# A diffusion block in f32 on one core: router and convolution rows transposed from normalized rows, the norm's affine part folded into columns, one product behind instead of two

## The chip, the core and the metric

The kernel runs on one core of one Trainium2 chip. Its engines work side by side, each through its own instructions in order, and wait for each other on semaphores: TensorE (matrix products and transposes), VectorE, ScalarE, GpSimd, and SyncE, which here only starts DMA transfers. The metric is the time of one execution on the device, in microseconds (us). The median of three runs of the kernel before is 2563.14 us (2562.48 to 2564.69). A measurement of this kernel can't tell a difference below some 0.2% from none.

## The reference

Two layers over 1024 tokens (and 256 context tokens in the first) of 1024 values, all f32. Cut to what the change touches:

```python
def layer_norm(x, w, b):            # mean and variance over the 1024 values of a row
    return (x - mu) * rsqrt(var + LN_EPS) * w + b

for l in range(2):
    u = modulate(h, m[0], m[1])                       # u = h * scale + shift, per column
    y = attn_gla_mixer(u, ...) if l == 0 else short_conv_mixer(u, ...)     # ends in @ w_out
    h = post_norm(h, m[2] * y, ln_w[l, 0], ln_b[l, 0])   # layer_norm(ALPHA*h + m[2]*y, w, b)
    tokens = modulate(h, m[3], m[4])
    y = hier_moe(tokens, router..., moe_w1, moe_w3, moe_w2)   # top 1 of 4 groups, top 2 of its 8 experts
    h = post_norm(h, m[5] * y, ln_w[l, 1], ln_b[l, 1])
```

The mixer of layer 1 is a gated convolution over three tokens: `u @ w_in`, the convolution, `@ w_out`. The router is a product of the modulated tokens with 4 + 32 columns. The two chosen experts of each token (w1, w3, w2 of 512 hidden values) are computed for gathered tokens; the weights of all experts, 6 MB each, stream in once per layer.

## The kernel before

The 1024 tokens are 8 tiles of 128 rows (t = 0 to 7). A product needs its input transposed, with the values on partitions: eight 128x128 transposes per tile on TensorE (line 585), then eight copies out of PSUM, which apply a scale and a shift per column (which is then per partition): ScalarE does four (`modulated`, line 1124), VectorE the other four (line 1367). "Columns" below means these eight.

The order of work on each engine is written out by hand, in one block per engine, and the engines meet in semaphores that count up. Those of this change:
- `out_mm`: output product of a tile done. `res`: residual written. `nrm`: rows normalized (mean and deviation applied, no weight and bias yet). `ln`: affine part applied too, rows stored in `hh`. `tile_T`: transposes done. `tile_a`, `tile_d`: columns done on ScalarE, VectorE. `comb`: combine products of a tile done. `wa2_in`: a group of small loads of the prologue.

Prologue. SyncE loads the adaLN weights in pieces (`ada_part`), VectorE sums them (line 1409), TensorE transposes the sums between units of the first projection. Small loads (convolution taps, sinks) stand in the same queue ahead of `ada_part(18)`.

Output product of layer 0 (`mixed_product`) and of layer 1 (`odd_product`). Per tile 32 passes of 128x512 (13.8 us). VectorE multiplies by the gate (line 1612), adds ALPHA times the input (1614), takes statistics of both halves (1594, 1595) and combines them (1597). ScalarE takes the root (1250), VectorE makes scale and shift (1602, 1604), ScalarE normalizes (1252). GpSimd multiplies by the norm's weight (1976) and adds its bias (1978) into `hh`, counts `ln`. TensorE transposes tile t - 2 in the middle of the product of tile t (`rows_T`) and multiplies with the router (`logits`, lines 880 and 882) at its end. Behind the loop stand the transposes and logits of tiles 6 and 7. SyncE writes each tile of `hh` to DRAM after its `ln`, then loads the next norm's parameters and the first 16 pieces of expert weights (1 MB each; 12 at once, four after the routing's order is known).

Routing and experts. VectorE computes the routing from the logits (lines 1620 to 1755) with some products on TensorE. GpSimd then gathers the rows of the first two blocks by indirect DMA (line 1987) from DRAM. TensorE transposes them and goes through 22 blocks, while SyncE refills weight pieces in slots that a block has freed.

Combine (`combined`) after the experts: per tile ALPHA times the saved rows plus the two experts' rows, by products with diagonal matrices (lines 1074 and 1076), then statistics on VectorE out of PSUM, the norm on ScalarE, the affine part on VectorE (`affine`, lines 1832 and 1834). In layer 0 the tile is then transposed and put through columns for the convolution (`stream_T`), tile t - 2 behind the combine of tile t. In SyncE's order, right after the combine's loads:

```python
sp.wait_ge(S("ln"), 2 * NT)     # all 8 tiles of the combine's affine
ln_params(1, 0)
router(1)
# then the convolution's weights wc, 2 x 3 loads of 512 KB; the first conv_chunk waits for them
```

`hh` lies in bigC, the rows between residual and norm in bigA (`zt0`, `zt1`; `zt` for the combine).

## Time and profile before

| | |
|---|---|
| median of 3 runs | 2563.14 us |
| profiled execution | 2561.24 us, its span 2559.4 us |
| TensorE busy | 2331.6 us, 91% of the span |
| VectorE, ScalarE, GpSimd busy | 30%, 16%, 11% |
| DMA while experts run | up to 421 GB/s over most slices |
| chain that ended last | TensorE 73%, DMA 12%, VectorE 7% |
| TensorE's clock over the span | 0.957 of full |

A busy share over the span says little here, since every stretch has its own limit. The chain of waits tells what a stretch hangs on: each row of it is a start, a length and the work that was waited for. The stretches that matter for the change: prologue (0 to 180 us), output product of layer 0 (630 to 784), routing (784 to 828), combine of layer 0 (1364 to 1431), output product of layer 1 (1775 to 1923), routing (1923 to 1968), final combine (2500 to 2559).

### The profile page before, as it was taken

How to read it: one execution, taken by the hardware profiler on the slowest of the kernel's cores; microseconds unless marked ns; L12 is line 12 of the kernel's file. 1: busy time of each engine (PE TensorE's matmuls, PEld its weight loads, DVE VectorE, ACT ScalarE, POOL GpSimd, SP SyncE). 2: the span in 40 equal slices, each digit the busy share in tenths (PEclk: the TensorE clock that was granted, in tenths of full speed). 3: DMA queues.
4: the chain of work that ended last, by engine and by line, in shares of the span. 5: the costliest groups of instructions: out<-in, count | busy, mean ns of one | idle time of the engine just before them, and what ended most of it. 6: DMA issues, size and time to landing. Idle time of an engine off the chain costs nothing.

```text
span 2559.4 us, 28344 instructions
## 1 busy us (share of the span) xinstructions
PE 2331.6 (91%) x10480; PEld 1179.1 (46%) x10480; DVE 759.8 (30%) x1661; ACT 418.6 (16%) x912; POOL 277.7 (11%) x341
## 2 busy tenths in 40 slices
PE   7989999998993999999998799997994999999887
PEld 3556448886553344344343344443553343443332
DVE  2783125555336111111115111111335111111115
ACT  2301324442111111011013100000120101101011
POOL 0000103222221100000000000000221000000000
PEclk9999999999995999999999899998995999999998
DMA  9871000002127999999965210101017999999956
GB/s 387 326 296 38 1 0 2 2 2 83 52 74 295 367 421 415 416 393 421 421 280 209 68 49 27 47 25 66 33 45 302 421 421 413 417 404 421 421 217 246
DMA packets 135165, 572.24 MB, mean 224 GB/s; under 512 B 24153, under 2 KB 49913, under 8 KB 82554
## 3 DMA queue, kind: packets, MB, share of 16 engines
q1 hardware_dynamic: 121786, 536.92, 52.8%
q0 software_dynamic: 13248, 33.57, 3.4%
q8 instruction: 82, 1.34, 0.2%
q14 instruction: 49, 0.40, 0.0%
HBM read 549.47 MB, written 35.65 MB: 229 GB/s over the span
## 4 chain that ended last, share of the span: by engine, by line
PE 73%; DMA 12%; DVE 7%; issue 3%; SPq 2%; ACT 1%; POOL 1%; DVEq 0%; POOLq 0%; ACTq 0%
PE bank L988 19%; PE bank L1060 13%; PE bank L1010 9%; DMA bigA<-in_moe_w 8%; PE bank L628 8%; PE bank L898 4%; PE bank L920 4%; PE bank L731 3%; DVE lnwb L1409 2%; PE bank L585 2%; SPq L406 2%; PE bank L882 1%; DMA bigA<-in_ada_w 1%; PE bank L745 1%; PE bank L714 1%
## 5 line engine op out<-in xcount | busy, mean ns | idle before, releaser
L988 PE MATMUL bank<-bigA,bigB 128*32 128x512 f32 (+2 forms) x1968 | 468.2, 601 | 12.6 <-DMA bigA<-in_moe_w 8.9
L1060 PE MATMUL bank<-bigB,bigA 128*128 128x512 f32 x768 | 331.5, 595 | 10.9 <-DMA bigA<-in_w_in_odd 10.9
L628 PE MATMUL bank<-bigC,bigB 128*128 128x512 f32 (+3 forms) x768 | 292.6, 537 | 0.0
L1010 PE MATMUL bank<-bigA,bigB 128*32 128x512 f32 (+2 forms) x1120 | 271.3, 601 | 18.6 <-DMA bigA<-in_moe_w 15.9
L988 PEld LDWEIGHTS bank<-bigA,bigB 128*32 128x32 f32 (+2 forms) x1968 | 162.4, 137 | 252.1 <-issue 246.7
L988 PE MATMUL bank<-bigC,bigB 128*128 128x512 f32 (+2 forms) x720 | 264.1, 597 | 8.8 <-DMA bigA<-in_moe_w 5.6
L1060 PEld LDWEIGHTS bank<-bigB,bigA 128*128 128x128 f32 x768 | 146.8, 191 | 195.2 <-issue 195.2
L628 PEld LDWEIGHTS bank<-bigC,bigB 128*128 128x128 f32 x768 | 142.8, 193 | 127.7 <-issue 119.7
L1124 ACT ACTIVATE bigB<-bank,small 128x128 f32<-128x128 f32 x288 | 107.2, 459 | 434.9 <-PE bank L585 434.8
L1010 PEld LDWEIGHTS bank<-bigA,bigB 128*32 128x32 f32 (+2 forms) x1120 | 98.9, 140 | 163.6 <-issue 159.4
L988 PEld LDWEIGHTS bank<-bigC,bigB 128*128 128x128 f32 (+2 forms) x720 | 91.0, 151 | 132.0 <-issue 128.0
L1992 POOL DMA_INDIRECT y_rows<-bigB,ints x44 | 44.3, 1007 | 904.8 <-DVE bigB L1784 904.8
L1784 DVE TENSOR_TENSOR bigB<-bank,gate 128x512 f32<-128x512 f32 x88 | 56.7, 686 | 268.0 <-PE bank L1010 268.0
L1775 DVE TENSOR_TENSOR bigB<-bigB,bank 128x512 f32<-128x512 f32 x44 | 30.2, 687 | 327.3 <-PE bank L988 327.3
L898 PE MATMUL bank<-bigB,bigA 128*128 128x512 f32 x256 | 114.2, 602 | 13.0 <-DMA bigB<-in_w_out_odd 13.0
L920 PE MATMUL bank<-bigB,bigA 128*128 128x512 f32 x256 | 115.2, 605 | 8.1 <-issue 8.1
L1266 ACT ACTIVATE bigB<-bank 128x512 f32<-128x512 f32 x44 | 26.3, 597 | 551.5 <-PE bank L988 551.5
L1976 POOL TENSOR_TENSOR bigA<-bigA,lnwb 128x1024 f32<-128x1024 f32 x16 | 37.6, 2347 | 648.2 <-ACT bigA L1252 648.2
L1876 DVE TENSOR_TENSOR bigA<-bank,bigA 128x512 f32<-128x512 f32 x16 | 11.1, 692 | 294.5 <-ACT bigA L1341 294.5
L1779 DVE COPY bigB<-bank 128x256 f32<-128x256 f32 x44 | 18.6, 424 | 267.0 <-PE bank L996 267.0
L1409 DVE SCALAR_TENSOR_TENSOR lnwb<-bigA,normw,lnwb 128x1024 f32<-128x1024 f32 x70 | 89.9, 1284 | 7.5 <-DMA bigA<-in_ada_w 3.3
L731 PE MATMUL bank<-bigB 128*128 128x128 f32 x608 | 83.8, 284 | 7.6 <-issue 6.6
(269 smaller groups left out, 2274.6 us busy)
## 6 DMA issues: line engine op xcount, KB each, us to landing
bigA<-in_moe_w SPq DMA_DIRECT2D x292, 1024.0 KB, 20.8
bigC<-in_moe_w SPq DMA_DIRECT2D x92, 1024.0 KB, 22.2
bigA<-in_ada_w SPq DMA_DIRECT2D x40, 1024.0 KB, 7.7
bigA<-y_rows SPq DMA_DIRECT2D x16, 1024.0 KB, 4.9
bigA<-in_w_in_odd SPq DMA_DIRECT2D x24, 512.0 KB, 6.1
bigA<-in_ada_w SPq DMA_DIRECT2D x4, 2048.0 KB, 12.4
bigA<-in_x SPq DMA_DIRECT2D x16, 512.0 KB, 11.1
bigC<-in_w_in_even SPq DMA_DIRECT2D x4, 2048.0 KB, 14.1
```

What stands on the lines that cost most here:

```text
L406: sp.dma_start(dst, src, **how).then_inc(S(name), 16)
L585: last = tp(bank(b + k // 4)[:, (k % 4) * P:(k % 4 + 1) * P], cols(src, n)[:, k, :], ident)
L628: last = mm(bank(n % 3)[:, 0:w], uT[:, k, t * P:(t + 1) * P], wring[:, g % 2, k, at_:at_ + w], start=(k == 0), stop=(k == KC - 1))
L731: last = mm(dst, sc[:, p % 3, g, k * P:(k + 1) * P], unit_p[:, p % 2, g, :], start=True, stop=True, skip_group_check=True)
L898: last = mm(bank(2 * (t % 2) + n), zT[:, k, t * P:(t + 1) * P], wout1[:, k, n * 512:(n + 1) * 512], start=(k == 0), stop=(k == KC - 1))
L920: last = mm(bank(2 * (t % 2) + n), lhs[:, k, :], wout[:, k0 + k, n * 512:(n + 1) * 512], start=(k0 + k == 0), stop=(k0 + k == KC - 1), ski ...
L988: last = mm(bank(m)[at_:at_ + w, :], xT[:, j, KC // 2 * h + k, at_:at_ + w], w13_at[SLOT_OF[m, h, q][0]][:, k, :], start=(h == 0 and k == ...
L1010: last = mm(bank(6 + n)[at_:at_ + w, :], gT[:, 2 * h + k, at_:at_ + w], w2_at[SLOT_OF[2, h, q][0]][:, k, n * 512:(n + 1) * 512], start=(h ...
L1060: last = mm(bank(3 * half + m), wc[:, j, m, k, :], u1T[:, k, half * 512:(half + 1) * 512], start=(k == 0), stop=(k == KC - 1))
L1124: last = go(dst[:, k, :], bank(b + k // 4)[:, (k % 4) * P:(k % 4 + 1) * P], ACT.Identity, bias=shift[:, k:k + 1], scale=scale[:, k:k + 1])
L1409: V(v.scalar_tensor_tensor(acc[:, r % 2], part, cond[:, k, 0:1], acc[:, r % 2], MUL, ADD))
L1784: v.tensor_tensor(yo[:, j, n * 512:(n + 1) * 512], bank(6 + n), gate[:, 1, n * 512:(n + 1) * 512], MUL)\
```

## The change

1. ScalarE writes normalized rows straight into `hh`, and TensorE transposes them from there as soon as `nrm` counts, before the affine part. The weight and bias of the norm go into the columns instead: a new table `lncol` holds, for three norms, weight x scale and bias x scale + shift. Four small loads (in the prologue, `wa2_in` up from 144 to 208) and six small VectorE operations make it.
2. The affine part of `hh` is applied in place afterwards: in the product loops by GpSimd, which now waits for the tile's transposes (`tile_T`); in the combine of layer 0 by VectorE, after the columns of the last tile.
3. The residual runs in halves of 512 columns, each behind its own count of `out_mm`, with its statistics behind it.
4. Transposes and logits are one tile behind the product instead of two. The router's bias product stands ahead of the wait for the columns.

Core of the diff (renumbered waits and renamed arguments left out):

```diff
+        lncol = col(48).rearrange("p (n i k) -> p n i k", n=3, i=2)
+        def normed_mod(i):
+            return lncol[:, i, 1], lncol[:, i, 0]
# SyncE, prologue, ahead of the ada parts from 18 on
+            for i, name in enumerate(("ln_w", "ln_b")):
+                load(lncol[:, 0:2, i], T[name][0].rearrange("j (p k) -> p j k", k=KC), "wa2_in")
+                load(lncol[:, 2, i], T[name][1, 0].rearrange("(p k) -> p k", k=KC), "wa2_in")
# TensorE
             def rows_T(l, t):
-                pe.wait_ge(S("ln"), 2 * l * NT + t + 1)
+                pe.wait_ge(S("nrm"), 2 * l * NT + t + 1)
...
             def logits(l, t):
+                dst = bank(5)[:, t * 36:(t + 1) * 36]
+                mm(dst, cc("ones")[0:1, :], rbias[0:1, :], start=True, stop=False)
                 pe.wait_ge(S("tile_a"), n + 1)
                 pe.wait_ge(S("tile_d"), n + 1)
-                dst = bank(5)[:, t * 36:(t + 1) * 36]
-                mm(dst, cc("ones")[0:1, :], rbias[0:1, :], start=True, stop=False)
...
-                    if n == 0 and t >= 2:
-                        rows_T(1, t - 2)
-                last.then_inc(S("out_mm"), 1)
-                if t >= 2:
-                    logits(1, t - 2)
+                    last.then_inc(S("out_mm"), 1)
+                    if n == 0 and t:
+                        rows_T(1, t - 1)
+                if t:
+                    logits(1, t - 1)
...
             for t in range(NT):
                 combined(0, t)
-                if t >= 2:
-                    stream_T(t - 2)
-            stream_T(NT - 2)
+                if t:
+                    stream_T(t - 1)
             stream_T(NT - 1)
# ScalarE
-                go(z[:, j], z[:, j] if src is None else src, ACT.Identity, bias=nm[:, j:j + 1], scale=rs[:, j:j + 1]).then_inc(S("nrm"), 1)
+                go(hh[:, t], src, ACT.Identity, bias=nm[:, j:j + 1], scale=rs[:, j:j + 1]).then_inc(S("nrm"), 1)
-                modulated(hT[l][:, t % 2], 6, mod_of(l, 1), "tile_a")
+                modulated(hT[l][:, t % 2], 6, normed_mod(2 * l), "tile_a")
             def combined(l, t):
-                if t >= 2:
-                    act.wait_ge(S("ln"), (2 * l + 1) * NT + t - 1)
-                ln(2 * l + 1, t, zt, banks[2 + t % 2][:, :])
+                ln(2 * l + 1, t, banks[2 + t % 2][:, :])
# VectorE, after the last mix_d
+            for i, (l, sub) in enumerate(((0, 1), (1, 0), (1, 1))):
+                shift, scale = mod_of(l, sub)
+                V(v.tensor_tensor(lncol[:, i], lncol[:, i], wide(scale.unsqueeze(1), [P, 2, KC]), MUL))
+                V.wait()
+                V(v.tensor_tensor(lncol[:, i, 1], lncol[:, i, 1], shift, ADD))
...
             def residual(l, t, z, x):
-                dve.wait_ge(S("out_mm"), l * NT + t + 1)
-                V(v.tensor_tensor(z[:, j], banks[j][:, :], gate[:, 0, :], MUL))
-                V.wait()
-                v.scalar_tensor_tensor(z[:, j], x, ALPHA, z[:, j], MUL, ADD).then_inc(S("res"), 1)
+                for n in range(2):
+                    part = slice(n * 512, (n + 1) * 512)
+                    dve.wait_ge(S("out_mm"), 2 * (l * NT + t) + n + 1)
+                    V(v.tensor_tensor(z[:, j, part], bank(2 * j + n), gate[:, 0, part], MUL))
+                    V.wait()
+                    last = v.scalar_tensor_tensor(z[:, j, part], x[:, part], ALPHA, z[:, j, part], MUL, ADD)
...
+                    half_stats(z[:, j], n)
...
             for t in range(NT):
                 combined(0, t)
-                if t >= 2:
-                    stream_T(t - 2)
+                if t:
+                    stream_T(t - 1)
+            stream_T(NT - 1)
+            for t in range(NT):
                 affine(0, t)
-            stream_T(NT - 2)
-            stream_T(NT - 1)
# GpSimd, product loops
-                pool.wait_ge(S("nrm"), n + 1)
-                G(pool.tensor_tensor(z[:, j], z[:, j], lnw, MUL))
+                pool.wait_ge(S("tile_T"), 2 * NT * l + t + 1)
+                G(pool.tensor_tensor(hh[:, t], hh[:, t], lnw, MUL))
                 G.wait()
-                pool.tensor_tensor(hh[:, t], z[:, j], lnb, ADD).then_inc(S("ln"), 1)
+                pool.tensor_tensor(hh[:, t], hh[:, t], lnb, ADD).then_inc(S("ln"), 1)
```

VectorE at the end of layer 0's combine, before: the last two tiles (L1367 columns, L1832 and L1834 the affine pair, L1594 to L1604 the norm), then the memsets ahead of the convolution.

```order
980 L1832 TENSOR_TENSOR bigA<-bigA,lnwb 128x1024 [waits nrm]
981 L1834 TENSOR_TENSOR bigC<-bigA,lnwb 128x1024 [waits dve_step]
982 L1594 BN_STATS small<-bank 128x6 [waits nrm,comb]
983 L1595 BN_STATS small<-bank 128x6
984 L1597 BN_AGGR small<-small 128x2 [waits dve_step]
985 L1602 RECIPROCAL small<-small 128x1 [waits sd]
986 L1604 SCALAR_TENSOR_TENSOR small<-small 128x1 [waits dve_step]
987 L1367 TENSOR_SCALAR bigB<-bank,small 128x128 [waits tile_T]
988 L1367 TENSOR_SCALAR bigB<-bank,small 128x128 x3
989 L1832 TENSOR_TENSOR bigA<-bigA,lnwb 128x1024 [waits nrm]
990 L1834 TENSOR_TENSOR bigC<-bigA,lnwb 128x1024 [waits dve_step]
991 L1367 TENSOR_SCALAR bigB<-bank,small 128x128 [waits tile_T]
```

The same place now (L1368 columns, L1854 and L1856 the affine pair; two of eight pairs shown):

```order
994 L1608 BN_AGGR small<-small 128x2 [waits dve_step,nrm]
995 L1613 RECIPROCAL small<-small 128x1 [waits sd]
996 L1615 SCALAR_TENSOR_TENSOR small<-small 128x1 [waits dve_step]
997 L1368 TENSOR_SCALAR bigB<-bank,small 128x128 [waits tile_T]
998 L1368 TENSOR_SCALAR bigB<-bank,small 128x128 x3
999 L1368 TENSOR_SCALAR bigB<-bank,small 128x128 [waits tile_T]
1000 L1368 TENSOR_SCALAR bigB<-bank,small 128x128 x3
1001 L1854 TENSOR_TENSOR bigC<-bigC,lnwb 128x1024 [waits nrm,ln_in]
1002 L1856 TENSOR_TENSOR bigC<-bigC,lnwb 128x1024 [waits dve_step]
1003 L1854 TENSOR_TENSOR bigC<-bigC,lnwb 128x1024 [waits nrm]
1004 L1856 TENSOR_TENSOR bigC<-bigC,lnwb 128x1024 [waits dve_step]
```

All affine pairs moved behind the columns of the last tile; the loop keeps only statistics, norm and columns.

TensorE at the end of layer 0's output product, before (L920 the last half of the product of tile 7, L585 transposes, L880 bias and L882 logits):

```order
735 L585 MATMUL bank<-cst,bigC 128x128 [waits tile_a,tile_d,ln,mix_a]
736 L585 MATMUL bank<-cst,bigC 128x128 x7
737 L920 MATMUL bank<-bigB,bigA 128x512 x8
738 L880 MATMUL bank<-bigB,cst 128x36 [waits tile_d,tile_a]
739 L882 MATMUL bank<-bigB,bigA 128x36 x8
740 L585 MATMUL bank<-cst,bigC 128x128 [waits tile_d,tile_a,ln]
741 L585 MATMUL bank<-cst,bigC 128x128 x7
742 L880 MATMUL bank<-bigB,cst 128x36 [waits tile_d,tile_a]
743 L882 MATMUL bank<-bigB,bigA 128x36 x8
744 L585 MATMUL bank<-cst,bigC 128x128 [waits tile_d,tile_a,ln]
745 L585 MATMUL bank<-cst,bigC 128x128 x7
746 L880 MATMUL bank<-bigB,cst 128x36 [waits tile_d,tile_a]
```

And now (L927 the product, L592 transposes, L886 bias, L890 logits):

```order
744 L592 MATMUL bank<-cst,bigC 128x128 [waits tile_a,tile_d,nrm,mix_a]
745 L592 MATMUL bank<-cst,bigC 128x128 x7
746 L927 MATMUL bank<-bigB,bigA 128x512 x8
747 L886 MATMUL bank<-bigB,cst 128x36
748 L890 MATMUL bank<-bigB,bigA 128x36 [waits tile_d,tile_a]
749 L890 MATMUL bank<-bigB,bigA 128x36 x7
750 L592 MATMUL bank<-cst,bigC 128x128 [waits tile_d,tile_a,nrm]
751 L592 MATMUL bank<-cst,bigC 128x128 x7
752 L886 MATMUL bank<-bigB,cst 128x36
753 L890 MATMUL bank<-bigB,bigA 128x36 [waits tile_d,tile_a]
754 L890 MATMUL bank<-bigB,bigA 128x36 x7
```

Behind the last product stand the logits of one tile and the transposes and logits of another; before, it was logits of three tiles and transposes of two. The transposes wait for `nrm` where they waited for `ln`.

## Rows read from the trace of the kernel before

**Rows 1.** Chain of waits before the convolution: start us, length us, what.

```profile
1417.63 0.34 SPq L406
...
1423.55 6.69 DMA bigA<-in_w_in_odd
...
1430.48 2.04 PE bank L1060 x2
```

**Rows 2.** Chain of waits, tile 6 in the loop, then layer 0's tail.

```profile
747.58 0.34 PE bank L880 x2
747.92 1.91 PE bank L882 x16
749.82 6.95 PE bank L920 x16
756.77 0.88 PE bank L585 x8
...
764.61 1.24 DVE bigA L1612
...
769.41 1.24 ACT bigA L1252
...
776.29 1.77 PE bank L585 x8
...
780.28 3.57 PE bank L882 x16
```

**Rows 3.** Chain of waits, the last logits of layer 1.

```profile
1919.49 3.57 PE bank L882 x16
```

**Rows 4.** Chain of waits, the first gather of each layer.

```profile
824.45 3.53 DMA bigB<-h_rows,ints
...
1963.96 4.23 DMA bigB<-h_rows,ints
```

**Rows 5.** Timeline of VectorE: start us, us, engine, line, operation [idle before, releaser].

```profile
113.84 5.36 DVE L1409 SCALAR_TENSOR_TENSOR lnwb<-bigA,normw,lnwb 128x1024 f32<-128x1024 f32 x4 [2.18 <-DMA bigA<-in_ada_w]
```

**Rows 6.** Timeline of TensorE in the prologue.

```profile
178.91 0.69 PE L640 MATMUL bank<-cst,lnwb 128*128 128x128 f32 x4 [1.97 <-DVE small L1398]
```

**Rows 7.** Timeline of VectorE in the combine of layer 0.

```profile
1372.98 1.22 DVE L1832 TENSOR_TENSOR bigA<-bigA,lnwb 128x1024 f32<-128x1024 f32 x1 [1.34 <-ACT bigA L1252]
...
1375.38 0.69 DVE L1594 BATCH_NORM_STATS2 small<-bank 128x6 f32<-128x512 f32 x1
```

**Rows 8.** Stretch view: us; PE, PEld, DVE, ACT, POOL busy; clock, DMA share, GB/s.

```profile
1381.70:1387.74 6.04, 6.04 (x23) 3.17 (x22) 5.22 (x12) 2.89 (x6) 0.00 (x0) 1.00 0.67 262
```

**Rows 9.** Timeline of TensorE at the combine's end.

```profile
1410.99 1.94 PE L585 MATMUL bank<-cst,bigC 128*128 128x128 f32 x16
1417.65 1.97 PE L585 MATMUL bank<-cst,bigC 128*128 128x128 f32 x8 [4.73 <-DVE bigC L1834]
```

**Rows 10.** The page's costliest groups: an operation on 512 columns.

```profile
L1876 DVE TENSOR_TENSOR bigA<-bank,bigA 128x512 f32<-128x512 f32 x16 | 11.1, 692 | 294.5 <-ACT bigA L1341 294.5
```

**Rows 11.** Stretch view, clock in both tails (third value from the end).

```profile
770.00:772.00 2.00, 0.00 (x0) 0.00 (x0) 0.65 (x3) 2.00 (x5) 1.27 (x1) 0.93 0.00 0
1908.00:1910.00 2.00, 0.00 (x0) 0.00 (x0) 1.60 (x6) 1.58 (x3) 0.05 (x1) 0.59 0.00 0
```

**Rows 12.** Timeline of GpSimd, the affine's second operation of tile 7.

```profile
773.14 2.34 POOL L1978 TENSOR_TENSOR bigC<-bigA,lnwb 128x1024 f32<-128x1024 f32 x1
```

**Rows 13.** Timeline of SyncE's queue, first expert weights of layer 0.

```profile
777.18 10.39 SPq L406 DMA_DIRECT2D bigA<-in_moe_w  x12
```

**Rows 14.** Stretch view, the end of the sixteen expert loads in both layers.

```profile
821.00:822.00 1.00, 1.00 (x7) 1.00 (x6) 0.64 (x4) 0.00 (x0) 0.00 (x0) 0.50 0.52 213
1961.00:1962.00 1.00, 1.00 (x6) 1.00 (x5) 0.26 (x2) 0.00 (x0) 0.00 (x0) 0.50 0.12 49
```

**Rows 15.** The gathers, line 1987, all 48.

```profile
DMA to landing us min/median/max: 2.2/10.9/11.9
```

**Rows 16.** Timeline of SyncE's queue: two loads of 768 pieces of 32 bytes.

```profile
2.60 1.42 SPq L406 DMA_DIRECT2D small<-in_ada_b  x2
```

More of the change, by code:

```diff
@@ L886, in last_rows @@
             def last_rows(l):
-                logits(l, NT - 2)
                 rows_T(l, NT - 1)
@@ L921, in half @@
                                       start=(k0 + k == 0), stop=(k0 + k == KC - 1), skip_group_check=True)
-                    return last
+                        if k0:
+                            last.then_inc(S("out_mm"), 1)
                 if t == 0:
@@ L939, in mixed_product @@
                 pe.wait_ge(S("mix_a"), t + 1)
-                if t >= 2:
-                    rows_T(0, t - 2)
-                half(4, mixT[:, t % 2]).then_inc(S("out_mm"), 1)
-                if t >= 2:
-                    logits(0, t - 2)
+                if t:
+                    rows_T(0, t - 1)
+                half(4, mixT[:, t % 2])
+                if t:
+                    logits(0, t - 1)
             for t in range(NT):
                 mixed_product(t)
-            rows_T(0, NT - 2)
             last_rows(0)
@@ L1244, in _, with ln @@
             go(rms, ms, ACT.Sqrt, bias=epsc[:, 1:2], scale=1.0 / DV).then_inc(S("rms_a"), 1)
-            def ln(norm, t, z, src=None):
+            def ln(norm, t, src):
                 j, n = t % 2, NT * norm + t
@@ L1342, in _ @@
             for t in range(NT):
[L1343 to L1346 removed]
+                if t:
+                    router_rows(1, t - 1)
+                ln(2, t, zt1[:, t % 2])
             router_rows(1, NT - 1)
@@ L1588, in _, with half_stats, ln_stats @@
                 last.then_inc(S("mix_d"), 1)
-            def ln_stats(norm, t, z):
-                j = t % 2
+            for i, (l, sub) in enumerate(((0, 1), (1, 0), (1, 1))):
[4 more added lines that the diff above has]
+            V.wait()
+            def half_stats(z, n):
+                last = v.bn_stats(bn6[:, 0, 6 * n:6 * n + 6], z[:, n * 512:(n + 1) * 512])
+                if n:
+                    V(last)
+            def ln_stats(norm, t):
                 if t >= 2:
                     dve.wait_ge(S("nrm"), NT * norm + t - 1)
-                v.bn_stats(bn6[:, 0, 0:6], z[:, 0:512])
-                V(v.bn_stats(bn6[:, 0, 6:12], z[:, 512:1024]))
                 V.wait()
-                v.bn_aggr(mv[:, j, :], bn6[:, 0, :]).then_inc(S("var"), 1)
+                v.bn_aggr(mv[:, t % 2, :], bn6[:, 0, :]).then_inc(S("var"), 1)
             def ln_scale(norm, t):
@@ L1608, in residual @@
                 j = t % 2
-                dve.wait_ge(S("out_mm"), l * NT + t + 1)
                 if t >= 2:
-                    dve.wait_ge(S("ln"), 2 * l * NT + t - 1)
-                V(v.tensor_tensor(z[:, j], banks[j][:, :], gate[:, 0, :], MUL))
-                V.wait()
-                v.scalar_tensor_tensor(z[:, j], x, ALPHA, z[:, j], MUL, ADD).then_inc(S("res"), 1)
-                dve.wait_ge(S("res"), l * NT + t + 1)
+                    dve.wait_ge(S("nrm"), 2 * l * NT + t - 1)
+                for n in range(2):
+                    part = slice(n * 512, (n + 1) * 512)
+                    dve.wait_ge(S("out_mm"), 2 * (l * NT + t) + n + 1)
+                    V(v.tensor_tensor(z[:, j, part], bank(2 * j + n), gate[:, 0, part], MUL))
+                    V.wait()
+                    last = v.scalar_tensor_tensor(z[:, j, part], x[:, part], ALPHA, z[:, j, part], MUL, ADD)
+                    if n == 0:
+                        V(last)
+                        V.wait()
+                    else:
+                        last.then_inc(S("res"), 1)
+                        dve.wait_ge(S("res"), l * NT + t + 1)
+                    half_stats(z[:, j], n)
             def moe(l):
@@ L1822, in combined @@
                 dve.wait_ge(S("comb"), l * NT + t + 1)
[L1823 removed]
+                for n in range(2):
+                    half_stats(banks[2 + t % 2], n)
+                ln_stats(2 * l + 1, t)
                 ln_scale(2 * l + 1, t)
             def affine(l, t):
[L1828 removed]
                 if t == 0:
                     dve.wait_ge(S("ln_in"), 32 * (2 * l + 2))
[L1831 to L1832 removed]
+                dve.wait_ge(S("nrm"), NT * (2 * l + 1) + t + 1)
+                V(v.tensor_tensor(hh[:, t], hh[:, t], lnw, MUL))
                 V.wait()
[L1834 removed]
+                v.tensor_tensor(hh[:, t], hh[:, t], lnb, ADD).then_inc(S("ln"), 1)
             def router_rows(l, t):
                 dve.wait_ge(S("tile_T"), 2 * NT * l + t + 1)
[L1839 removed]
+                modulated(hT[l][:, t % 2], 6, normed_mod(2 * l), "tile_d")
             for t in range(NT):
[L1842 to L1843 removed]
+                if t:
+                    router_rows(0, t - 1)
                 dve.wait_ge(S(f"x_in{t % 2}"), 16 * (t // 2 + 5 - t % 2))
                 residual(0, t, zt0, xin[:, t % 2])
[L1846 removed]
+                ln_stats(0, t)
                 ln_scale(0, t)
[L1848 removed]
             router_rows(0, NT - 1)
```

65 lines of the change are left out of this document (23 added, 42 removed).

## Prediction

> **What bounds the kernel now.** I read the page first, then the chain of waits over the span, then chain and timelines in the four places that the diff touches. TensorE is nearly always busy, so an edit counts only where TensorE waits. In the touched code it waits at three places, twice at the same kind. (1) Before the convolution: the chain goes from VectorE's last affine to SyncE's queue at 1417.63, to the convolution weights, whose load is on the chain from 1423.55, to the first convolution product at 1430.48 [rows 1]. (2) After each layer's last output product, until the router logits of the last tile are there [rows 2, 3]. (3) Behind the routing, for the first gathered rows [rows 4]. A fourth, smaller one is in the prologue: VectorE waits for an ada weight load at 113.84, and TensorE waits for VectorE's sums at 178.91 [rows 5, 6].
>
> **Convolution start: the affine pairs leave the combine loop.** Before, each tile's two affine instructions stand inside the loop. A pair starts at 1372.98, and the instruction behind it at 1375.38, so a pair costs 2.40 [rows 7]. In the changed order all eight pairs stand behind the column work of the last tile. SyncE may load router and convolution weights only when the 16th "ln" is counted, and the diff leaves that wait alone.
> - Does the loop get shorter in return? One iteration, from 1381.70 to 1387.74, has TensorE busy for 6.04 of 6.04 us [rows 8]. VectorE is busy for 5.22 and often seems to set the pace in the chain, but taking 2.40 from it leaves TensorE's 6.04. So I take no gain from the loop.
> - The last combine products end at 1410.99 [rows 9], now as then. The norm takes 3.56 from statistics to normalized rows: in the tail of layer 0 from 764.61 plus two operations of 1.24 to 769.41 plus 1.24 [rows 2]. So rows are there at 1414.6. Transposes take 0.88 [rows 2] and the first half of the column work, which runs on both engines, about 1.3: 1416.8. Before, the transposes of this tile came at 1417.65 [rows 9], so this side alone is some 3 us early.
> - Then 8 x 2.40 + 0.1 = 19.3: the last affine ends at 1436.1. Before it ended at 1417.6. The 12.85 us from there to the product [rows 1] follow unchanged. **+18.5.** Nothing hides it: TensorE has no other work before the convolution. If the clock has fallen at the last transposes (1.77 for 0.88), it is +19.4.
>
> **Tails of the two output products.** Inside the loops nothing gets longer: the same products, transposes and logits, one product behind instead of two. Transposed rows are wanted 9.2 us or more after the product's end: logits 0.34 + 1.91, then half a product, 6.95 [rows 2]. The norm needs 4.4 (below), 4.8 less. VectorE has long idle stretches there and SyncE's x loads still wait for the residual.
> - One more tile's transposes and logits now stand before the last product's end: 0.88 + 0.34 + 1.91 = 3.13 [rows 2]. It ends at 764.6 + 3.1 = 767.7.
> - Only the second half of the residual is left then: two operations of 0.69 [rows 10], statistics of one half 0.69, and the 2.27 that remain of the 3.56 (3.56 less two halves of statistics). With the gaps 4.4: normalized rows at 772.1. Before, 764.61 to 770.65, 6.04.
> - The transposes don't wait for GpSimd's affine any more: 0.88, columns 1.58 (778.06 to 779.64), eight logit products 1.91. The bias product now stands ahead of the wait. 776.5 at full clock. Before, the last logits ended at 780.28 + 3.57 = 783.85 [rows 2]: 7.3 earlier. At half clock (1.77 and 3.57 for 0.88 and 1.91) it is 779.1: 4.8 earlier. Between the two lies what the clock does over an idle of 2.2 us. In this trace it fell late in an idle stretch in one layer (0.93 granted over 770 to 772, so 2.4 GHz for most of it) and early in the other (0.59 over 1908 to 1910, mostly 1.2 GHz) [rows 11]. I keep both. Layer 1's tail is the same (logits to 1923.06) [rows 3].
>
> **But the gather's queue starts later.** GpSimd's affine of the last tile now waits for the transposes: 773.0 + 2 x 2.35 + 0.1 = 777.8, where it ended at 775.48 [rows 12]. Behind it stand the write of these rows, the norm parameters and sixteen expert loads of 1 MB, the first at 777.18 [rows 13]. They start 2.3 later (3.2 at half clock). Before, they kept the DMA engines busy to about 821.5 in layer 0 and 1961.1 in layer 1 [rows 14], and the first gather started just behind them, at 824.45 and 1963.96, landing 3.53 and 4.23 later [rows 4]. Now the loads end at 823.8 to 824.7 while the gather is issued 4.8 to 7.3 earlier, at 817.2 to 819.7, into a full queue. Gathers in the expert phase, under full load, land 10.9 us after issue in the median [rows 15]. So I let it land 1.5 us (its own packets) behind the loads: 825.3 to 826.2 instead of 827.98, and 1964.9 to 1965.8 instead of 1968.19. That is -1.8 to -2.7 and -2.4 to -3.3. **I take -2.3 and -2.8, together -5.1**; the rest of the earlier routing is lost in front of the gather. Bounds for the two: -14.6 (not held, full clock) and 0 or slightly above (held for 10.9). What follows in the expert phase hangs on slots that the first block frees, so it shifts as a whole.
>
> The Trainium skill bears on this place ("DMA: Bandwidth & Descriptors", Queues, rings and completion order): a DMA engine takes turns between the queues that have work, packet by packet. By that rule a gather isn't kept behind a long queue of loads, and the case "not held" below would hold. The trace's 10.9 against 3.53 speaks for a good deal of holding, whoever takes turns.
>
> **Prologue.** Four loads of 32-byte pieces come before the ada loads, on the same queue. Two loads with more pieces took 1.42 for issue [rows 16]; these four have 768 pieces together, as one of those two. VectorE already waits 2.18 for the ada load at that point, and TensorE 1.97 for VectorE at the end of that stretch [rows 5, 6], so a delay goes through. Between 0 and 3; **I take +1.3**, four issues of some 0.4 less what overlaps.
>
> **At nothing:** the six small operations on the columns fall into VectorE's idle stretch before the first residual; the final combine keeps its order on VectorE, which sets it; ACT's dropped wait there held nothing up.
>
> **Sum.** +18.5 - 5.1 + 1.3 = +14.7. The profiled execution took 2561.24 (span 2559.4 and 1.84 around it), so 2575.9 for it; the median of the runs is 1.9 above it, so I forecast 2563.14 + 14.7 = 2577.8, rounded 2578.
>
> **Rivals.**
> - *Gather not held.* It lands 3.5 to 4.2 behind its issue whatever else is queued, and both tails give 4.8 to 7.3. 18.5 + 1.3 - 12.1 = +7.7: 2571 (to 2568.3 at full clock). For it: the gather has a queue of its own. Against it: the 10.9 under load.
> - *Gather held for its full 10.9.* From an issue at 818.5 that is 829.4, 1.4 later than before; in layer 1 issue at 1957.9 gives 1968.8, 0.6 later. Then +18.5 + 1.3 + 2 = +21.8: 2585. Against it: the loads run out after 6 us, so the load that holds it is gone.
> - *The combine loop is VectorE's* (the not-slower end). The chain of waits in that stretch names VectorE most of the time, and there each iteration would fall by 2.40 when the pair goes, until loads or products stop it. With six full iterations that is 14.4 back: 18.5 - 14.4 + 1.3 - 5.1 = +0.3: 2563.4. It decides from the point where TensorE's time per iteration is under about 3.6 instead of 6.04. Against it: 6.04 busy of 6.04 [rows 8].
> - *The closer distance stalls the product loops* (the change doesn't do what it says): transposed rows would be late if the norm took over 9.2 instead of 4.4 after the product; each us of lateness costs 14 us over both loops: 2592 for the first. Nothing in the rows shows such a delay.
>
> **Chances.** Forecast 0.62, not held 0.18, held fully 0.10, loop of VectorE 0.05, stalled loops 0.03, something else 0.02. Below 2569 lie the loop case and the best end of "not held"; above 2584 the held and stalled cases: 2569 to 2584, with some 0.2 outside. A measurement of this kernel can't tell less than 0.2%, 5.1 us, from no change. Faster by more needs a gain of 24 against the sum: 0.02. Within 5.1: the loop case and an edge of "not held", 0.08. Slower: 0.90.
>
> **What would show it.** In the changed profile: eight affine pairs back to back on VectorE right before the convolution weights' load, with TensorE idle for some 34 us before its first convolution product (else the first term is wrong); the combine iterations still 6.04 apart; last logits 5 to 7 us earlier relative to the start of the product loop; GpSimd's last affine 2 to 3 us later; the first gather issued while expert loads still land, and taking more than 4.3 us; the ada wait at 113.84 longer by one or two. A combine iteration under 5 us, or a gather landing within 4.3 us of its issue, would make the forecast wrong.

## The result, and the profile of the changed kernel

The changed kernel takes 2580.27 us in the median of four runs (2579.57 to 2582.03), the kernel before, run beside it, 2562.81 (2561.36 to 2564.69). The ratio is 1.0069, with a 95% interval of 1.0051 to 1.0086: slower by 0.7%. Measured a second time it was 2582.51 against 2562.61, 1.0079 (1.0066 to 1.0093). The forecast was 2578, 2569 to 2584. The profiled execution has a span of 2577.7 against 2559.4, 18.3 more, where the sum gave 14.7.

The profile's list of the costliest groups names the main place. The last part of the row is TensorE's idle time before the group and what ended most of it.

```profile
L1067 PE MATMUL bank<-bigB,bigA 128*128 128x512 f32 x768 | 332.5, 596 | 33.3 <-DMA bigA<-in_w_in_odd 33.3
```

Before, the same products waited 10.9. The chain of waits over that stretch (start us, length us, what) answers to [rows 1, 9]:

```profile
1410.28 1.73 PE bank L1083 x4
...
1415.66 1.17 PE bank L592 x8
...
1418.23 1.14 DVE bigC L1854
1419.39 1.22 DVE bigC L1856
...
1436.16 1.24 DVE bigC L1856
1437.41 0.34 SPq L410
...
1442.01 0.59 SPq L410
...
1443.36 6.50 DMA bigA<-in_w_in_odd
...
1450.11 10.21 PE bank L1067 x17
```

These rows are one line of dominoes, in which only the eight pairs are new. The last combine products end at 1412.0 (1411.0 before), the last tile's rows are transposed at 1415.66, its columns are there at 1418.2, and then VectorE does sixteen affine operations in a row until 1437.4. SyncE, which counts them, sends the parameters, the router's weights and only then the convolution's. The first product is at 1450.11, 19.6 later than before. Of this 1.0 was there already at the end of the combine, so 18.6 arose here.

The tail of layer 0 in the timelines of TensorE, GpSimd and SyncE's queue (start us, us, engine, line, operation, idle before and its releaser):

```profile
773.78 1.97 PE L592 MATMUL bank<-cst,bigC 128*128 128x128 f32 x8 [2.30 <-ACT bigC L1257]
777.35 3.63 PE L890 MATMUL bank<-bigB,bigA 128*128 128x36 f32 x16 [1.03 <-ACT bigA L1129]
778.26 2.35 POOL L1998 TENSOR_TENSOR bigC<-bigC,lnwb 128x1024 f32<-128x1024 f32 x1
782.30 11.78 SPq L410 DMA_DIRECT2D bigA<-in_moe_w  x12
```

The last logits end at 780.98 instead of 783.85 [rows 2], although the last product ends 4.7 later. But GpSimd's affine ends at 780.6 instead of 775.5 [rows 12], and the expert loads begin at 782.30 instead of 777.18 [rows 13]. What that does to the first gather is in the chain and in the stretch view (its last two values are the DMA engines' share and GB/s):

```profile
821.88 7.36 DMA bigB<-h_rows,ints
...
832.85 12.48 PE bank L995 x45
```

```profile
815.00:821.00 6.00, 5.02 (x24) 4.85 (x23) 4.90 (x25) 0.00 (x0) 0.00 (x0) 0.50 1.02 426
821.00:827.00 6.00, 0.00 (x0) 0.00 (x0) 2.24 (x5) 0.00 (x0) 4.79 (x7) 0.50 1.00 414
827.00:833.00 6.00, 2.13 (x10) 1.73 (x12) 1.37 (x4) 1.70 (x5) 6.00 (x11) 0.50 0.20 75
```

The gather is issued 2.6 earlier than before, into DMA engines that are full, and takes 7.36 instead of 3.53 [rows 4]. The first block starts at 832.85, where it started at 831.59. In layer 1 it is the same: the gather takes 7.77 instead of 4.23, and TensorE waits 9.55 for the gathered rows. The first row is from the chain, the others are from the timeline.

```profile
1979.43 7.77 DMA bigB<-h_rows,ints
```

```profile
1932.57 1.36 PE L592 MATMUL bank<-cst,bigC 128*128 128x128 f32 x8 [2.30 <-ACT bigC L1257]
1935.53 3.63 PE L890 MATMUL bank<-bigB,bigA 128*128 128x36 f32 x16 [1.03 <-ACT bigA L1129]
...
1987.24 1.97 PE L592 MATMUL bank<-cst,bigB 128*128 128x128 f32 x8 [9.55 <-DMA bigB<-h_rows,ints]
```

In the prologue, SyncE's queue and VectorE's wait, against [rows 5]:

```profile
107.96 1.09 SPq L410 DMA_DIRECT2D small<-in_ln_w  x2
109.09 0.94 SPq L410 DMA_DIRECT2D small<-in_ln_b  x2
```

```profile
115.82 5.36 DVE L1410 SCALAR_TENSOR_TENSOR lnwb<-bigA,normw,lnwb 128x1024 f32<-128x1024 f32 x4 [4.18 <-DMA bigA<-in_ada_w]
```

The wait grew by 2.0. The same row of TensorE in the first output product comes 1.5 later (642.51 instead of 640.99).

### The profile page after: what moved, and what is told of

Its sections match the earlier page's. It is cut to its first block, busy times and chain, and to the rows that moved or that the text cites. A ratio compares the mean times of both kernels' runs of the same rounds, so it can differ in the third digit from the quotient of the medians.

```text
span 2577.7 us, 28377 instructions
## 1 busy us (share of the span) xinstructions
PE 2330.8 (90%) x10480; PEld 1174.1 (46%) x10480; DVE 771.6 (30%) x1699; ACT 419.2 (16%) x912; POOL 280.7 (11%) x341
## 4 chain that ended last, share of the span: by engine, by line
PE 75%; DMA 10%; DVE 8%; SPq 2%; issue 2%; ACT 2%; POOL 1%; DVEq 0%; POOLq 0%; ACTq 0%
PE bank L995 19%; PE bank L1067 13%; PE bank L1017 10%; PE bank L635 8%; DMA bigA<-in_moe_w 7%; PE bank L905 4%; PE bank L927 4%; PE bank L592 3%; PE bank L738 3%; DVE lnwb L1410 2%; SPq L410 2%; PE bank L890 1%; PE bank L1083 1%; PE bank L721 1%; PE bank L752 1%
## 5 line engine op out<-in xcount | busy, mean ns | idle before, releaser
L927 PE MATMUL bank<-bigB,bigA 128*128 128x512 f32 x256 | 115.0, 604 | 8.3 <-issue 8.3
L1996 POOL TENSOR_TENSOR bigC<-bigC,lnwb 128x1024 f32<-128x1024 f32 x16 | 37.6, 2353 | 672.5 <-PE bank L592 672.5
## 6 DMA issues: line engine op xcount, KB each, us to landing
bigC<-in_w_in_even SPq DMA_DIRECT2D x4, 2048.0 KB, 13.6
```

What stands on the lines that cost most here:

```text
L927: last = mm(bank(2 * (t % 2) + n), lhs[:, k, :], wout[:, k0 + k, n * 512:(n + 1) * 512], start=(k0 + k == 0), stop=(k0 + k == KC - 1), ski ...
```

## The experiments

Each kernel is the changed one with the edit shown. The kernel before had a median of 2561.6 beside the first four runs, 2565.6 (2560.3 to 2567.0) beside the next four and 2562.6 beside the last three, so ratios carry over better than times.

The traces give a steadier measure than the times. Nine of the traces are of kernels that are the same up to the first output product, and yet the same row in it (four transposes behind a wait of 0.78) starts anywhere from 641.05 to 644.32. From that row to the end of the span the changed kernel takes the same in every trace that should be alike:

| from that row to the end of the span | us |
|---|---|
| before | 1918.4 |
| changed, changed again, small loads late | 1935.2, 1935.4, 1935.2 |
| pairs back in the loop; on GpSimd | 1919.5; 1918.7 |
| last four prefetched loads behind the gathers | 1938.4 |
| convolution loads at the combine; with the pairs on GpSimd | 1904.0; 1904.5 |
| expert loads ahead | 1931.8 |
| residual whole | 1938.3 |
| all three edits, GpSimd; VectorE | 1904.7; 1904.6 |

Each other kernel has one trace, so differences of a few tenths say nothing.

**The pairs back in the loop**, each tile's behind its own columns:

```diff
                 if t:
                     stream_T(t - 1)
+                    affine(0, t - 1)
             stream_T(NT - 1)
-            for t in range(NT):
-                affine(0, t)
+            affine(0, NT - 1)
```

> The changed kernel with VectorE's affine pairs of layer 0's combine put back into the loop, each pair behind the columns of its tile; all else as changed. Theory: the wait for the last affine sets the start of the convolution. The last pair then ends 2.4 us behind the last columns, at about 1420.7 instead of 1437.4 in the changed kernel's trace, and the first convolution product follows 12.7 us later, near 1433.4 instead of 1450.1: 16.7 us less in all, some 2563.6. Combine iterations stay at 6.04 us, since TensorE fills them. Rival (the combine loop is VectorE's): iterations grow to some 8.4 and less than 5 us is won. Rival (the loss at the convolution has another cause, such as the clock or the small loads): no more than 5 us is won.

2565.32, ratio 1.0012 (1.0002 to 1.0022); one of the ten runs took 6273.76, and the median is 2564.93 without it. The chain before the convolution:

```profile
1421.27 1.15 DVE bigC L1854
...
1422.43 1.24 DVE bigC L1856
...
1429.64 6.66 DMA bigA<-in_w_in_odd
...
1436.54 3.75 PE bank L1067 x4
```

The start is 13.6 earlier in a profile that ran 1.9 later at the end of the expert stage, so 15.5 of the 18.6 are gone. That is 1.2 less than expected: in this order the pair of tile 6 (1417.60 to 1419.99) still stands between the last norm and the last columns. An iteration still takes 6.03 (1401.89 to 1407.92): the pairs were free in the loop, since TensorE sets its pace, and outside it they cost nearly their whole length.

**The pairs on GpSimd**, each behind its tile's transposes, taken from VectorE:

```diff
+            pool.wait_ge(S("ln_in"), 64)
+            for t in range(NT):
+                pool.wait_ge(S("tile_T"), NT + t + 1)
+                G(pool.tensor_tensor(hh[:, t], hh[:, t], lnw, MUL))
+                G.wait()
+                pool.tensor_tensor(hh[:, t], hh[:, t], lnb, ADD).then_inc(S("ln"), 1)
```

> The changed kernel with the affine part of layer 0's combine on GpSimd, tile by tile behind the transposes, as in the product loops. Theory: GpSimd needs 4.8 us per tile, under the 6.04 of an iteration, and ends 4.8 us behind the last transposes (1416.8): 1421.6, so the convolution starts near 1434.4 instead of 1450.1: 15.7 less, some 2564.6. Rival (GpSimd and VectorE hold each other up when they work side by side on SBUF): operations on GpSimd take clearly more than 2.35 or VectorE's statistics and columns more than 0.69 and 1.37, iterations get longer than 6.04, and less than 12 us is won.

2565.86, 1.0028 (1.0001 to 1.0055; one of the ten runs took 2597.47, which widens it), the first convolution weights on the chain from 1428.83 instead of 1443.36. It matters that the pairs don't pile up, not who does them.

**The last four prefetched loads behind the first gathers:**

```diff
                         sp.wait_ge(S("h_out"), 16 * NT * (l + 1))
+                        sp.wait_ge(S(f"xg_in{l}_0"), 16)
+                        sp.wait_ge(S(f"xg_in{l}_1"), 16)
```

> The changed kernel, but in both layers the 13th expert load and those behind it wait until the first two gathers have landed. Theory: the gather is held by the expert loads queued before it. With four loads (10 us of transfer) taken out of its way the queue is empty when it is issued, it lands 3.5 to 4.3 us after issue instead of 7.4 and 7.8, and each first block starts 3.5 us earlier: 7 us less, some 2573. The four loads end near 837, well ahead of the second block, so nothing is lost. Rival (the longer landing is the gather's own, for instance by its descriptors being written while VectorE or GpSimd works): it still takes 7 us and the time stays at 2580. Rival (the loads are wanted early): the second block waits for weights and the win is given back, 2578 to 2583.

2582.57, 1.0079 (1.0062 to 1.0095): no gain, 10 above what was expected. Its chain, SyncE's queue, and TensorE's timeline:

```profile
822.13 3.59 DMA bigB<-h_rows,ints
...
829.34 15.69 PE bank L997 x59
```

```profile
828.60 3.70 SPq L410 DMA_DIRECT2D bigC<-in_moe_w  x4
836.35 11.76 SPq L410 DMA_DIRECT2D bigA<-in_moe_w  x8
```

```profile
908.46 5.34 PE L997 MATMUL bank<-bigA,bigB 128*32 128x512 f32 x32 [3.42 <-DMA bigA<-in_moe_w]
...
940.78 3.64 PE L1019 MATMUL bank<-bigA,bigB 128*32 128x512 f32 x32 [0.37 <-DMA bigA<-in_moe_w]
```

The same place in the changed kernel:

```profile
940.65 3.64 PE L1017 MATMUL bank<-bigA,bigB 128*32 128x512 f32 x32 [2.26 <-DMA bigA<-in_moe_w]
```

The theory of the gather holds: with nothing queued ahead it lands in 3.59, and the first block starts 3.5 earlier. But that lead is gone at 940.78, against 940.65 in the changed kernel. While the loads waited, the DMA engines stood idle (0.42 and 0.31 busy over 815 to 821 and 821 to 827), and TensorE waits for just that later, at 908. In layer 1 more is lost than was gained: the gather lands in 3.48, TensorE waits 3.43 at 2068.99, and at 2101.29 this kernel is 2.4 behind the changed one, both counted from the first output product of the layer. So the first block does not set the pace of this stage; the loads of its weights do, from some 80 us behind its start on.

**The four small loads later**, behind the prologue's last weight loads:

```diff
+            for i, name in enumerate(("ln_w", "ln_b")):
+                load(lncol[:, 0:2, i], T[name][0].rearrange("j (p k) -> p j k", k=KC), "wa2_in")
+                load(lncol[:, 2, i], T[name][1, 0].rearrange("(p k) -> p k", k=KC), "wa2_in")
             sp.wait_ge(S("acc_ok"), 10)
```

> The changed kernel with the four small loads of norm weights and biases moved behind the adaLN loads and the last projection weights. Theory: they delay the adaLN loads by some 2 us, and VectorE's wait in front of its sums passes 1.6 us of it on; with them gone VectorE waits 2.2 instead of 4.2 at that place, the first output product starts 1.6 us earlier and the time is 1.6 less, some 2578.7. Rival: TensorE's and VectorE's slack swallow it, no change.

2579.11, 1.0070 (1.0054 to 1.0087). VectorE's wait is back at 2.24 and TensorE is 2.05 earlier at 126 us. By the medians 1.2 is won and by the ratios nothing, so the rival (slack swallows it) isn't out. Nor do the traces give a size: with the small loads early the wait is 3.85 to 5.55 in nine traces, with them late 2.24, 2.88 and 3.82 in three.

**SyncE's order before the convolution**, which shows who waited for what. It changes three things at once: what SyncE waits for, which loads go first, and where VectorE's pairs stand.

```diff
-                sp.wait_ge(S("ln"), 2 * NT)
-                ln_params(1, 0)
-                router(1)
+                sp.wait_ge(S("comb"), NT)
                 w_odd = T["w_in_odd"][0].rearrange("(p k) (m c n) -> p m k c n", k=KC, m=3, n=P)
                 for c in range(2):
                     for m in range(3):
                         load(wc[:, c, m], w_odd[:, m, :, c, :], f"wc_in{c}")
+                router(1)
+                sp.wait_ge(S("ln"), 2 * NT)
+                ln_params(1, 0)
```

with VectorE's `for t in range(NT): affine(0, t)` moved behind its four memsets.

> The changed kernel, except that SyncE waits for the eighth combine product (comb) and not for the sixteenth ln before it issues the first six convolution loads, sends the two norm-parameter loads and the router loads behind them, and VectorE does its eight affine pairs behind the four memsets instead of ahead of them. Theory 1 (the cost of the moved affine pairs is nothing but SyncE's in-order wait in front of the convolution's loads): the last combine product of layer 0 ends near 1412.0, the loads go out then and the first set lands 7.9 us later (1442.01 to 1449.9 in the changed kernel), so the convolution starts near 1420 instead of 1450.11, 29 to 30 us earlier, and the time is 2580.3 - 29.7 = 2551, below the kernel before the change (2561.6 on this chip). Theory 2 (VectorE's eight pairs, 19.2 us, cost by themselves, since the convolution's first VectorE step stands behind them): the convolution starts early, but TensorE waits for VectorE in its second or third group until the pairs are done at about 1438, and 7 us or more of it is lost: 2558 or more.

2550.11, ratio 0.9947 (0.9931 to 0.9962): 30 below the changed kernel, and faster than the one before. Its chain, the row of these products among the costliest groups, and VectorE's timeline:

```profile
1411.15 1.73 PE bank L1084 x4
...
1412.90 0.61 SPq L410
...
1414.26 6.72 DMA bigA<-in_w_in_odd
...
1421.23 4.60 PE bank L1068 x5
```

```profile
L1068 PE MATMUL bank<-bigB,bigA 128*128 128x512 f32 x768 | 332.1, 595 | 3.5 <-DMA bigA<-in_w_in_odd 3.5
```

```profile
1419.48 1.23 DVE L1855 TENSOR_TENSOR bigC<-bigC,lnwb 128x1024 f32<-128x1024 f32 x1 [0.36 <-DVE bigA L1887]
...
1437.50 1.23 DVE L1857 TENSOR_TENSOR bigC<-bigC,lnwb 128x1024 f32<-128x1024 f32 x1
1445.52 0.69 DVE L1898 TENSOR_TENSOR bigA<-bank,bigA 128x512 f32<-128x512 f32 x1 [6.80 <-ACT bigA L1344]
```

VectorE does the same sixteen operations about 1.2 later than in the changed kernel, and nobody waits: its first step of the convolution comes 6.8 after them, and TensorE waits for nothing else in all 768 products. The products need the weights and the transposed columns, not the affine rows. So the pairs cost nothing by themselves (theory 1 against theory 2).

Counted from the end of the last combine product, the first convolution product starts after 38.1 in the changed kernel, 19.5 before, and 8.4 here. Of the 29.7 won over the changed kernel 25.4 are the wait for the 16th `ln`, and 4.6 are the six loads that no longer stand ahead (issued from 1437.41 to 1442.01 there); the load takes 0.2 more here. So the kernel before paid 11 of the same kind. No run makes this edit to the kernel before; that it would win those 11 is argued from the chain [rows 1].

**The same with the pairs on GpSimd:**

> As the run before (first convolution loads behind the eighth combine product), with the eight affine pairs on GpSimd, each tile's behind its own transposes. Theory 1: the same start of the convolution, near 1420, and 2551, no difference from the run before, since the pairs stand in nobody's way in either. Theory 2 (the pairs on VectorE cost by themselves): this kernel is 7 us or more faster than the run before. GpSimd and VectorE may hinder each other in the combine loop; in the run with the pairs on GpSimd alone an iteration stayed at 6.03.

2548.89, 0.9943 (0.9927 to 0.9958): 1.2 from the run before, not 7.

**Three and four expert loads ahead of the last tile's ln:**

```diff
+                ahead = ((6, 7, 8), (0, 1, 2, 3))[l]
                 for t in range(NT):
+                    if t == NT - 1:
+                        for n in ahead:
+                            piece(n)
                     sp.wait_ge(S("ln"), 2 * l * NT + t + 1)
...
+                    if n in ahead:
+                        continue
```

> The changed kernel, except that SyncE issues three (layer 0) and four (layer 1) of the first twelve expert loads ahead of its wait for the last tile's ln, some 14 us earlier, so that the load queue runs empty before the first gather is issued. Theory 1 (the gather is held by the loads queued ahead, 7.4 and 7.8 us against 3.5 where nothing is queued, and loads that start later are what ate the tails' gain): the gather lands in 3.5 in both layers, the first expert block starts 3.7 us earlier in each, and since no transfer time is lost (as it was when the loads waited for the gather) the expert stage keeps it: 2580.3 - 7.5 = 2573. Theory 2 (the expert stage is paced by its weight stream from 839 on, whatever the start of the first block): the first block starts earlier and TensorE waits that much longer near 905 to 940: 2580 +- 1.

2576.83, 1.0046 (1.0032 to 1.0060). Chain and TensorE's timeline:

```profile
822.77 3.61 DMA bigB<-h_rows,ints
...
830.00 15.21 PE bank L1006 x57
```

```profile
908.14 3.64 PE L1006 MATMUL bank<-bigA,bigB 128*32 128x512 f32 x32 [2.52 <-DMA bigA<-in_moe_w]
939.22 3.64 PE L1028 MATMUL bank<-bigA,bigB 128*32 128x512 f32 x32 [0.83 <-DMA bigA<-in_moe_w]
```

The gather lands in 3.61. This profile is 0.95 late at the tail's transposes (774.73), so the first block's lead is 832.85 - 830.00 + 0.95 = 3.8, as expected. At 939 it is 940.65 - 939.22 + 0.95 = 2.4; in layer 1, the first block starts 54.6 behind the transposes instead of 58.2, and at the same kind of row, at 2095.68, 3.15 of these 3.6 are left. The truth is between the theories: of 7.4 gained at the first blocks 5.5 are kept at those rows. Less of it reaches the end. The whole kernel is 3.4 shorter by the traces and 3.5 by the medians. Layer 0 ends its expert stage 2.5 earlier, counted from the output product (1341.77 - 643.45 against 1343.34 - 642.51), but the convolution starts no earlier (1451.10 - 643.45 = 807.65 against 1450.11 - 642.51 = 807.60; in the second trace of the changed kernel it is 808.69). 1.2 of the 2.5 went into eight products right behind the stage, which took 6.75 instead of 5.53: the granted clock behind their first half was 0.59 instead of 0.94. The rest is no more than the spread of that stretch. Layer 1 keeps 3.3 to its last expert row.

**The residual over the whole tile again:**

```diff
+                dve.wait_ge(S("out_mm"), 2 * (l * NT + t) + 2)
+                V(v.tensor_tensor(z[:, j], banks[j][:, :], gate[:, 0, :], MUL))
+                V.wait()
+                v.scalar_tensor_tensor(z[:, j], x, ALPHA, z[:, j], MUL, ADD).then_inc(S("res"), 1)
...
                 for n in range(2):
-                    part = slice(n * 512, (n + 1) * 512)
-                    dve.wait_ge(S("out_mm"), 2 * (l * NT + t) + n + 1)
...
                     half_stats(z[:, j], n)
```

> The changed kernel with the residual of a tile done over 1024 columns at once behind both halves of the output product, as before the change (two operations of 1.23 us and two half statistics, instead of the first half's four operations under the second half's product). Theory 1 (each output product's tail is on the path): in each tail 2 x (1.23 - 0.70) + 0.69 of statistics = 1.8 us more between the end of the last product and the last transposes, so 2580.3 + 3.5 = 2583.8. Theory 2 (the tail is hidden, the load queue decides when the gather lands and the first block starts): the transposes start 1.8 later and the first block does not move by as much, 2580 to 2581.

2583.48, 1.0081 (1.0067 to 1.0095). The last transposes of layer 0 wait 4.06 instead of 2.30, 1.76 later, as expected; at the end of the expert stage 0.7 of it is left, at the end of layer 1's 2.6 more are there. The medians are 3.2 apart and the traces 3.1. The ratios are only 0.0002 to 0.0012 apart (against 1.0079 and 1.0069), which is within the noise. So the 1.8 per tail is shown; that the halves are worth some 3 us in all is likely, from one trace, and not settled by the times.

**The edits that had paid, together:** first convolution loads behind the combine, expert loads ahead, small loads late; the pairs on GpSimd in the first, on VectorE in the second.

> The changed kernel with the edits that paid, together: first convolution loads behind the eighth combine product, the eight affine pairs on GpSimd, three and four expert loads ahead of the last tile's ln, and the four small norm-column loads behind the prologue's last weight loads. If the gains are independent: 2548.9 (the loads at the combine with the pairs on GpSimd) - 3.5 (the expert loads ahead: 2576.8 against 2580.3) - 1.2 (the small loads late: 2579.1 against 2580.3) = 2544, 0.9925 to 0.993 of the kernel before. If the expert loads' gain depends on the weight stream (0 where the first block starts earlier for another reason): 2548.

> As the run before, with the eight affine pairs on VectorE behind the memsets: 2550.1 - 3.5 - 1.2 = 2545.4, and no more than 2 us from the run before, since in neither does anybody wait for the pairs.

2546.58, 0.9939 (0.9926 to 0.9953), and 2546.48, 0.9934 (0.9920 to 0.9948): 16 below the kernel before and 36 below the changed one on the same chip. But next to the runs with only the loads at the combine, at 0.9943 and 0.9947, the gain is 0.0004 and 0.0013, inside the intervals, where 4.7 us were expected. In the traces there is none: 1904.7 and 1904.6 from the first output product on, against 1904.5 and 1904.0. The 3.5 that the expert loads won alone doesn't show here: in layer 1, from the first output product to the last expert row, these two take 703.0 and 703.7, the two without the edit 703.0 and 703.1, and the run with the expert loads ahead alone 700.7. Why it is lost isn't shown. What is shown is that nearly all of the gain is the order before the convolution.

**The changed kernel again:**

> The changed kernel once more, on the chip of the two runs before, so that their gains are read against it and not across chips: 2580.3, 1.0069 of the kernel before.

2582.51, with a profiled span of 2577.7.

## Why the prediction was right, and where its sum was off

Slower was right, and so was its main cause. By the steps of the sum:

| step | predicted | measured |
|---|---|---|
| convolution start | +18.5 | +18.6 |
| tail of layer 0 | -2.3 | -0.7 |
| tail of layer 1 | -2.8 | -1.95 |
| prologue | +1.3 | +1.5 |
| convolution stage | 0 | +0.8 |
| sum | +14.7 | +18.3 |

The measured ones are shifts between two profiled executions, rounded: the convolution as above; layer 0 by the same row at the end of the expert stage (1342.51, now 1343.34) less the prologue; layer 1 by the first output product (1774.99, now 1795.42) and the last expert row (2480.93, now 2499.41); the convolution stage is 20.43 - 19.63. Two shifts of 0.2 stand outside the table and cancel (combine of layer 0 +0.2, final combine -0.2). The prologue's +1.5 and the convolution stage's +0.8 are not clear of the spread between traces: where the output product starts, the nine traces of kernels that are the same up to there differ by 3.3, and the convolution stage takes 344.4 to 345.6 in all twelve traces of changed kernels. So the number came out partly by luck: the sum was 3.6 short, and the median only 2.3 above the forecast, since its margin between profiled execution and median (1.9) didn't recur (0.7).

**Convolution start.** "8 x 2.40", "I take no gain from the loop" and "nothing hides it" held: iterations stay at 6.04, the pairs take 1418.14 to 1437.39, and the load follows as before. The rival of a loop set by VectorE is out, by this trace and by the run with the pairs back in the loop. What the prediction named but didn't price was that the wait needn't be there: 30 us against the changed kernel, 11 of which the kernel before paid already.

**Tails.** The mechanism was right, the two sizes were not; this is the step of the sum that was off, by 2.45 of 3.6. The routing chain was early as the half-clock case has it: the norm ended 4.5 behind the product, the clock was granted at 0.50 over 774 to 776, logits took 3.63, GpSimd's affine ended 5.1 later (3.6 without the prologue's delay, where the prediction had 3.2 at half clock). Counted from the output product of its layer, the first block was then 0.3 earlier in layer 0 and 1.4 in layer 1 (1.26 less 1.52 of the prologue; 1990.81 less 1971.79 and less 20.43), where 2.3 and 2.8 were predicted. "I let it land 1.5 us behind the loads" had the loads end at 824.7. Full engines lasted to 828 (426, 381, 332, then 119 GB/s in the four stretches of 1 us from 825), so the landing was 829.24, which is 827.7 without the prologue's delay, against 825.3 to 826.2. The prediction had moved the end of the stream by the shift of its start and left out that the gathered rows and the loads share one bandwidth: two gathers of 0.5 MB at 426 GB/s are 2.5 us, an estimate that closes the gap and that no run isolates. Second, "it shifts as a whole" is wrong as a rule: two runs moved the first block by 3.5 and 3.8 and kept 0 and 2.4 of it near 940. Here it cost the sum nothing, since the expert stages ended 0.7 and 1.95 earlier, a little more than their first blocks.

The rivals *not held* and *held for its full 10.9* are both out: 7.36 and 7.77 with the loads still running, 3.59 and 3.61 in layer 0 of the two runs where the queue had run empty. The Trainium skill ("DMA: Bandwidth & Descriptors", Queues, rings and completion order) has the DMA engines take turns between queues packet by packet, which would let a gather through. These gathers, issued some 6 us before the DMA engines ran empty, landed only then: in effect this trace disagrees, and why isn't shown here.

**Prologue and the rest.** The four loads take 2.1 of SyncE's queue, and VectorE's wait grew by 2.0, as the prediction's range of 0 to 3 allows; what of it reaches the end isn't shown. *Stalled product loops* didn't come: TensorE has no wait for normalized rows or for columns inside the loops.

## What to carry to other kernels

When work is moved behind a loop, look for who counts it: an in-order queue that waits for its last piece holds everything behind it, also what needs none of it. Ask of each such wait what the next transfer truly needs; here the answer was worth 30 us where the change itself cost 18, because the kernel before had been paying 11 for the same order. And where a stage lives on a stream of loads, an earlier first product is kept only as far as the stream gets earlier too. Here, leaving the DMA engines idle to let the gathers pass gave nothing and cost 3 us by the traces, while starting the stream earlier won 3.4. And gains that were measured alone need a run together: here they didn't add up.

## What the hardware showed that I had not expected

The same kernel has two speeds in layer 1's routing, by the granted clock. The stretch view of the first profile of the changed kernel, and of its second:

```profile
1948.00:1954.00 6.00, 5.19 (x32) 4.86 (x30) 0.87 (x4) 0.00 (x0) 0.00 (x0) 0.78 1.02 427
```

```profile
1948.00:1954.00 6.00, 6.00 (x24) 5.75 (x25) 0.48 (x3) 0.00 (x0) 0.00 (x0) 0.50 1.01 425
```

At 0.50 granted (1.2 GHz) sixteen small products take 3.60 (from 1952.36), at 1.00 granted (2.4 GHz) 1.95 (from 1951.23), and the routing's end is 2.4 further from its start (25.5 against 23.2). TensorE had been idle for 8.3 before both. But the first blocks stand at 1990.81 and 1991.10: the gather is issued later and held less (it takes 5.28 instead of 7.77, and TensorE waits 7.07 for it instead of 9.55). So the wait on the full queue swallowed the slower routing. Where the expert loads go ahead this cover is gone: from the last transposes to the first block it is 54.6 with the routing at the higher clock (the run with the expert loads ahead) and 56.8 at the lower (all three edits, pairs on GpSimd).

All 48 gathers of both layers, most of them issued while expert loads run, took 10.8 us in the median, with the longest at 12.2, much as before the change [rows 15]:

```profile
DMA to landing us min/median/max: 2.2/10.8/12.2
```
